# Sample attention: key pages waited for by halves, value pages released and loaded in two parts

## The chip, the cores and the metric

The kernel runs on one core of a Trainium2 chip. Its time is the device time of one execution in microseconds (us); the time before is 2310.9 us, the median of three runs (2310.64 to 2313.34). The engines are TensorE (PE in the profile, its weight loads PEld), VectorE (DVE), ScalarE (ACT), GpSimd (POOL) and SyncE (SP). An "SPq" row is SP issuing a transfer; POOL issues transfers too.

## The reference, cut to what matters

One decoder layer over a prompt of 1024 tokens and a sample group of 8 sequences with 8 new tokens each. The change concerns the attention of the sample group: each sequence attends to 1024 cached rows (8 pages of 128 rows, found through a page table) and its 8 new ones, over 8 heads of 64.

```python
k_past = cache_k[l][page_table].reshape(Bs, -1, ATT_HEADS, HEAD_DIM)
v_past = cache_v[l][page_table].reshape(Bs, -1, ATT_HEADS, HEAD_DIM)
...
s = jnp.einsum('bqhd,bkhd->bhqk', q, k).astype(jnp.float32) * (HEAD_DIM ** -0.5)
s = s + jnp.transpose(dq, (0, 2, 1))[..., None] - jnp.transpose(dk, (0, 2, 1))[:, :, None, :]
s = jnp.where(mask, s, -jnp.inf)
p = jax.nn.softmax(s, axis=-1)
return jnp.einsum('bhqk,bkhd->bqhd', p.astype(v.dtype), v)
```

dq and dk are running sums of a forget gate. Everything else in the layer (a combined input projection, a gated convolution, causal pooling, the gates, the output projection, two layer norms and a SwiGLU) is large matrix products and element work, and it is the same in both kernels.

## The kernel before, in words

The program is written engine by engine; each engine's list of instructions is fixed, and semaphores tie the lists together. Phases in order of time: set-up and modulation (to about 80 us), the prompt's attention with its projections (to about 472 us), the sample attention (472 to 665 us), and from there on matrix products of split float32 numbers, which keep TensorE busy to the end.

The sample attention goes sequence by sequence, b = 0 to 7; turns 0 to 6 are a hardware loop, turn 7 is written out. For each sequence there are four things in memory: `kpage` (8 key pages of 128x512), `kt_s` (the keys transposed), `decs` (the decay terms, then scores, then probabilities, 128 x 520) and `vpage` (8 value pages and the 8 new rows). All of them have one buffer. In turn b, TensorE does in this order:

1. the scores of b from `kt_s` (L1788);
2. groups 0 to 4 of the transposes of the keys of b + 1 (L1777; a group is four 128x128 transposes into one of two PSUM banks, even groups are copied out by ScalarE, odd ones by VectorE, L889 and L1233). Groups 0 to 3 read pages 0 to 3 (the first half), groups 4 to 7 pages 4 to 7;
3. the transposes of the probabilities of b (L1796, L1798), which wait for the softmax;
4. group 5;
5. the values of b: 8 matrix products over pages (L1809) and one over the new rows (L1810);
6. groups 6 and 7, then the fold of the heads (L1815).

The softmax of b is on VectorE: add and maximum (L1240), three small ones (L1243 to L1245), then `queries` of b + 1 (L1227, L1229) and the copies of groups 1 and 3, then the sum of the rows and the scaling (L1253 to L1257). ScalarE copies group 0, does the exponential (L895) and copies groups 2 and 4.

SP loads, per turn of its own loop: the first half of the key pages of a sequence after groups 0 to 3 of the one before, four decay transfers (L476) after the probabilities were transposed, and the second half of the key pages after group 7 of the one before. Both halves count on one semaphore, `kpg_in`, and TensorE waits before group 0 and again before group 4, both times for all eight pages. POOL loads all eight value pages (L366) and the new rows (L656) of b + 1 once the values of b are done (`ov_done`); TensorE waits for all of them before L1809. Before its loop POOL also splits the prompt's attended values (L631, L632).

Of the kernel before, what the change touches and what calls it, by code (L numbers as in the profile page):

```python
# [33 lines left out]
DB, DS = 8, 8  # L34
NS = DB * DS
T = 1092
TU = NP + NS
# [3 lines left out]
HP = H // 2  # L41
PAST, PAGE = 1024, 128
NPG = PAST // PAGE
# [4 lines left out]
NT = HALF // P  # L48
# [50 lines left out]
def build(nc, a, out):  # L99
    with ExitStack() as ctx:  # L100
# [167 lines left out]
        def scratch(name, shape):  # L268
# [14 lines left out]
            z_done e_done lf_done lf_tr lf_copied lfs_out lfnew_in scan_done ndp_out nds_out early_out  # L283
            q_done k_done v_done qhi_done ql_done kv_done kl_done tok_tr tok_copied kst vst vl_done decay0_in decay1_in
            s_done mx_done p_done pn_done tr_done pth_done ptl_done o_done o_copied ol_done
            kpg_in vpg_in dec_in vnew_in kt_tr kt_act kt_dve qbd_zero qbd_done ss_done sm_done se_done sp_done
            pt_tr pt_act pt_dve ov_done om_done fold_done sah_done sal_done pad_done
            cb_done cc_done ch_done cc_copied u_done y_done chi_done clo_done ul_done ul_tr ul_copied ul_out
            pcopied pf_done phi_done plo_done pt2_tr pt2_copied pt2_out mhi_done mlo_done
            wo_ev xr0_in xr1_in ysum_done mean_done d_done sq_done var_done sd_done xn_done xa_done  # L290
# [67 lines left out]
        def apart(eng):  # L358

            eng.sem_inc(s["idle"], 1)  # L360
# [18 lines left out]
        def _(sp):  # L379
# [73 lines left out]
            wunit(U_BRA + 2, (U_BRA + 2) % RING, tiles(a["w_br_attn"][0], 0, 2 * P), 4)  # L453

            sp.wait_ge(s["s_done"], NTILE * (HP - 1))
            for half in range(2):
                page_loads(sp, 0, kpage, "cache_k", s["kpg_in"], range(4 * half, 4 * half + 4))
            sp.wait_ge(s["o_copied"], NTILE * HP)
            sp.wait_ge(s["vl_done"], HP)
            sp.wait_ge(s["vst"], 32 * HP)  # L460
# [4 lines left out]
            def key_loads(b, half):  # L465
                sp.wait_ge(s["kt_tr"], b * 2 * HP - HP * (1 - half))
                apart(sp)
                page_loads(sp, b, kpage, "cache_k", s["kpg_in"], range(4 * half, 4 * half + 4))

            def decay_loads(b):  # L470
                if not isinstance(b, int) or b:
# [82 lines left out]
        def _(pool):  # L554
# [96 lines left out]
            nc.gpsimd.memset(qbd[:, :], 0.0).then_inc(s["qbd_zero"], 1)  # L651

            pool.wait_ge(s["pt_in"], 16)
            def sample_values(b):
                page_loads(pool, b, vpage, "cache_v", s["vpg_in"])
                pool.dma_start(vpage[0:DS, NPG, :],  # L656
                               out["v_sample"][0, bass.ds(b, 1)].rearrange("o t h d -> t (o h d)")).then_inc(s["vnew_in"], 16)

            sample_values(0)
            for p in range(HP):  # L660
                attended(p)
            with pool.Fori(1, DB) as b:
                pool.wait_ge(s["ov_done"], b)
                apart(pool)
                sample_values(b)
            one(U_BRA + 2)
            three(U_BRA + 3, (U_POOL - U_BRA - 3) // 3)
            for u_ in range(U_POOL, U_POOL + 4):
# [36 lines left out]
        def _(act):  # L705
# [176 lines left out]
            act.wait_ge(s["o_done"], HP * QT)  # L882
            act.wait_ge(s["kst"], 32 * HP)
            act.wait_ge(s["vst"], 32 * HP)
            nc.scalar.copy(ahi[:, :, TU:T], zeros[:, :].rearrange("p (a b) -> p a b", a=NT)).then_inc(s["pad_done"], 1)

            def keys_t(b, g):
                act.wait_ge(s["kt_tr"], b * 2 * HP + (g + 1))
# [153 lines left out]
        def _(dve):  # L1042
# [172 lines left out]


            dve.wait_ge(s["o_copied"], NTILE * HP)
            V.tensor_copy(alo[:, :, TU:T], zeros[:, :].rearrange("p (a b) -> p a b", a=NT)).then_inc(s["pad_done"], 1)
            dve.wait_ge(s["qbd_zero"], 1)
            dve.wait_ge(s["kst"], 32 * HP)  # L1220
            dve.wait_ge(s["vst"], 32 * HP)
# [13 lines left out]
            def sample(b, more):  # L1235
                dve.wait_ge(s["dec_in"], b * 64 + 64)
                link(V.tensor_tensor(decs[:, KH:LR], decs[:, KH:LR], maskn[:, :], ALU.add))
                dve.wait_ge(s["ss_done"], b + 1)
                apart(dve)
                link(V.tensor_tensor_reduce(decs[:, :], flat(psA)[:, 0:LR], decs[:, :], 1.0, NEG, ALU.add, ALU.max,  # L1240
                                            rowmax[:, 0:1]))

                link(V.tensor_scalar(other[0:NS, :], rowmax[NS:2 * NS, 0:1], -1.0, None, ALU.mult))  # L1243
                link(V.tensor_scalar(other[NS:2 * NS, :], rowmax[0:NS, 0:1], -1.0, None, ALU.mult))
                V.scalar_tensor_tensor(out=negmax[:, 0:1], in0=rowmax[:, 0:1], scalar=-1.0, in1=other[:, :], op0=ALU.mult,  # L1245
                                       op1=ALU.min).then_inc(s["sm_done"], 1)
# [12 lines left out]
                V.tensor_copy(ptrs[0:DS, NPG // 2, :], psB[0:DS, 1, 0:P]).then_inc(s["pt_dve"], 1)  # L1259
                if more:  # L1260
                    keys_t(b + 1, 5)

                dve.wait_ge(s["ov_done"], b + 1)
# [258 lines left out]
        def _(pe):  # L1522
# [247 lines left out]
            def keys_t(b, groups):  # L1770
                for g in groups:
                    if g % HP == 0:
                        pe.wait_ge(s["kpg_in"], b * (16 * NPG) + 16 * NPG)
                    if g >= 2:
                        pe.wait_ge(s["kt_dve" if g % 2 else "kt_act"], b * HP + g // 2)
                    for j in range(4):
                        m = tr(mi[g % 2][:, j * P:(j + 1) * P], kpage[:, 4 * (g // HP) + j, (g % HP) * P:(g % HP + 1) * P], ident[:, :])  # L1777
                    m.then_inc(s["kt_tr"], 1)

            def sample(b, more):  # L1780
# [17 lines left out]
                tr(psB[0:DS, 1, 0:P], decs[:, KH:LR], ident[:, :]).then_inc(s["pt_tr"], 1)  # L1798
                if more:
                    keys_t(b + 1, [5])  # L1800
                pe.wait_ge(s["vpg_in"], b * (16 * NPG) + 16 * NPG)
                pe.wait_ge(s["vnew_in"], b * 16 + 16)
                pe.wait_ge(s["pt_act"], b + 1)
                pe.wait_ge(s["pt_dve"], b + 1)
                hpg = NPG // 2
                for g in range(hpg):
                    for half in range(2):
                        rows = slice(half * NS, (half + 1) * NS)
                        mm(psB[rows, 2, :], ptrs[:, g, rows], vpage[:, half * hpg + g, :], start=g == 0, stop=half == 0 and g == hpg - 1)  # L1809
# [31 lines left out]
            branch(0, U_BRA, (s["ss_done"], DB), (s["sal_done"], DB), ((s["sal_done"], DB), (s["ol_done"], HP), (s["pad_done"], 2)))  # L1841

            pe.wait_ge(s["mA"], 4)
            pe.wait_ge(s["mB"], 4)
# [168 lines left out]
```

## Time and profile before

| what | value |
|---|---|
| median of 3 runs | 2310.9 us |
| the profiled execution's own time | 2310.69 us |
| its span, first to last instruction | 2309.0 us |
| TensorE busy | 2106.8 us, 91% |
| VectorE, GpSimd, ScalarE busy | 35%, 27%, 16% |
| mean granted TensorE clock | 0.953 |

The page cuts the span in 40 slices of 57.7 us. TensorE's busy tenths are 9 nearly everywhere; the slices of the sample attention read 6, 7, 6, 8, and the granted clock is 8 in each of them, against 9 behind it. Busy shares are means over phases; what counts in the sample attention is who waits for whom inside a turn, and that is read from its own stretch of the trace.

### The profile page before, as it was taken

What the parts mean: (1) busy time and instruction counts of PE and PEld (TensorE: products, weight loads), DVE (VectorE), ACT (ScalarE), POOL (GpSimd) and SP (SyncE); (2) the same over time, 40 slices, a digit from 0 to 9 for tenths busy, and PEclk for the clock granted to TensorE, in tenths of its full rate; (3) what the DMA queues carried; (4) which work ended last, traced back from release to release, by engine and by line L of the source; (5) the groups of instructions that cost most, each with busy time, mean ns of one, the idle gap of its engine ahead of it and who ended that gap; (6) DMA issues with size and microseconds to landing.
All of it is one profiled execution on the core that took longest, in us unless ns stands there. A gap on an engine that the chain in (4) does not pass through costs nothing.

```text
span 2309.0 us, 32811 instructions
## 1 busy us (share of the span) xinstructions
PE 2106.8 (91%) x13074; PEld 1986.3 (86%) x13074; DVE 798.3 (35%) x1328; ACT 367.6 (16%) x645; POOL 627.3 (27%) x474
## 2 busy tenths in 40 slices
PE   3899999867689999999979999699999999999996
PEld 3788888644469999999979999499999999999996
DVE  1525445533210023212532154714342243422426
ACT  1424344321110000000110100500000000000003
POOL 4220210041222222222222234042222222222233
PEclk8899999688889999999989999799999999999998
DMA  7861112045621111111111122011111111111112
GB/s 246 298 197 47 38 47 75 1 156 180 208 78 46 46 37 46 37 46 45 34 38 46 39 92 66 10 46 46 45 39 43 45 45 45 45 37 45 46 37 78
DMA packets 172992, 164.06 MB, mean 71 GB/s; under 512 B 13438, under 2 KB 136786, under 8 KB 172779
## 3 DMA queue, kind: packets, MB, share of 16 engines
q1 hardware_dynamic: 152155, 132.47, 18.6%
q0 software_dynamic: 6656, 17.08, 2.3%
q10 hardware_dynamic: 14104, 13.43, 1.8%
q8 instruction: 56, 0.92, 0.2%
q14 instruction: 21, 0.17, 0.0%
HBM read 149.03 MB, written 14.03 MB: 71 GB/s over the span
## 4 chain that ended last, share of the span: by engine, by line
PE 83%; DVE 7%; SPq 3%; issue 2%; DMA 2%; ACT 2%; POOLq 0%; POOL 0%; ACTq 0%; DVEq 0%
PE psA L1537 11%; PE psA L1543 11%; PE psA L1541 11%; PE psB L1543 10%; PE psB L1541 10%; PE psB L1537 10%; PE psB L1635 2%; PE psB L1638 2%; PE psB L1639 2%; DMA kpage<-in_cache_k 2%; PE ps L1777 1%; PE psB L1809 1%; PE ps L1702 1%; PE psA L1719 1%; PE psA L1720 1%
## 5 line engine op out<-in xcount | busy, mean ns | idle before, releaser
L597 POOL CAST whi<-raw 128x1024 fp32r<-128x1024 f32 x139 | 147.4, 1060 | 1289.2 <-PE psA L1537 607.0
L598 POOL TENSOR_TENSOR wlo<-raw,whi 128x1024 fp32r<-128x1024 f32 x139 | 336.8, 2423 | 11.2
L1537 PE MATMUL psA<-hhi,whi 128*128 128x364 f32 x1176 | 267.4, 337 | 47.1 <-DVE hlo L1403 20.2
L1541 PE MATMUL psA<-hlo,whi 128*128 128x364 f32 x1176 | 264.7, 334 | 0.0
L1543 PE MATMUL psA<-hhi,wlo 128*128 128x364 f32 x1176 | 264.2, 334 | 0.0
L1537 PEld LDWEIGHTS psA<-hhi,whi 128*128 128x128 f32 x1176 | 208.5, 193 | 53.6 <-issue 39.8
L1543 PE MATMUL psB<-hhi,wlo 128*128 128x364 f32 x1056 | 233.3, 329 | 0.0
L1541 PE MATMUL psB<-hlo,whi 128*128 128x364 f32 x1056 | 233.2, 329 | 0.0
L1537 PE MATMUL psB<-hhi,whi 128*128 128x364 f32 x1056 | 232.2, 328 | 0.0
L1543 PEld LDWEIGHTS psA<-hhi,wlo 128*128 128x128 f32 x1176 | 208.8, 192 | 0.0
L1541 PEld LDWEIGHTS psA<-hlo,whi 128*128 128x128 f32 x1176 | 208.7, 192 | 0.0
L1543 PEld LDWEIGHTS psB<-hhi,wlo 128*128 128x128 f32 x1056 | 183.7, 188 | 0.0
L1537 PEld LDWEIGHTS psB<-hhi,whi 128*128 128x128 f32 x1056 | 183.1, 188 | 0.0
L1541 PEld LDWEIGHTS psB<-hlo,whi 128*128 128x128 f32 x1056 | 183.1, 188 | 0.0
L1423 DVE TENSOR_TENSOR ft<-psB,sil 128x1092 f32<-128x1092 f32 x22 | 28.5, 1296 | 412.6 <-PE psB L1543 397.0
L1009 ACT CAST ahi<-ft 128x1092 fp32r<-128x1092 f32 x22 | 24.3, 1107 | 473.2 <-PE psB L1543 312.5
L1537 PE MATMUL psA<-ahi,whi 128*128 128x364 f32 x366 | 81.8, 332 | 8.5 <-DVE alo L1373 8.5
L1635 PE MATMUL psB<-hhi,whi 128*128 128x364 f32 x240 | 84.7, 353 | 2.0 <-DVE qlo L1121 2.0
L1777 PE MATMUL ps<-ident,kpage 128*128 128x128 f32 x256 | 49.4, 357 | 36.7 <-DMA kpage<-in_cache_k 35.4
L1296 DVE TENSOR_TENSOR part<-psA,sg 128x1092 f32<-128x1092 f32 x8 | 10.4, 1296 | 209.4 <-PE psA L1543 209.4
L1541 PE MATMUL psA<-alo,whi 128*128 128x364 f32 x366 | 81.1, 330 | 0.0
L1543 PE MATMUL psA<-ahi,wlo 128*128 128x364 f32 x366 | 81.1, 330 | 0.0
(328 smaller groups left out, 3312.2 us busy)
## 6 DMA issues: line engine op xcount, KB each, us to landing
raw<-in_w_in SPq DMA_DIRECT2D x53, 512.0 KB, 3.9
ada<-in_ada_w SPq DMA_DIRECT2D x12, 2048.0 KB, 13.8
raw<-in_w_gate_up SPq DMA_DIRECT2D x44, 512.0 KB, 3.8
kpage<-in_cache_k SPq DMA_DIRECT2D x64, 256.0 KB, 3.6
vpage<-in_cache_v POOLq DMA_DIRECT2D x64, 256.0 KB, 4.0
raw<-in_w_down SPq DMA_DIRECT2D x22, 512.0 KB, 3.7
x_keep<-xt SPq DMA_DIRECT2D x1, 4368.0 KB, 18.0
xr<-x_keep ACTq DMA_DIRECT2D x8, 546.0 KB, 4.9
```

The lines of the kernel that those rows point to most:

```text
L597: link(nc.gpsimd.tensor_copy(whi[slot][:, 0:n, :], raw[slot][:, 0:n, :]))
L598: nc.gpsimd.tensor_tensor(wlo[slot][:, 0:n, :], raw[slot][:, 0:n, :], whi[slot][:, 0:n, :].bitcast(F32), ALU.subtract).then_inc(s["w_split ...
L1009: nc.scalar.copy(to, ft[k][:, :]).then_inc(s["fhi_done"], 1)
L1423: V.tensor_tensor(c3(ft[k][:, :]), cols(psB), c3(sil[k][:, :]), ALU.mult).then_inc(s["ft_done"], 1)
L1537: m = mm(ps[:, c, 0:CH], whi[slot][:, b, :], hi[:, k, c * CH:(c + 1) * CH], start=first, stop=False)
L1541: mm(ps[:, c, 0:CH], whi[slot][:, b, :], lo[:, k, c * CH:(c + 1) * CH], start=False, stop=False)
L1543: m = mm(ps[:, c, 0:CH], wlo[slot][:, b, :], hi[:, k, c * CH:(c + 1) * CH], start=False, stop=last)
L1635: m = mm(bank[:, 0:CH], whi[slot][:, k, :], hhi[:, k, at], start=k == 0, stop=False)
L1638: mm(bank[:, 0:CH], whi[slot][:, k, :], hlo[:, k, at], start=False, stop=False)
L1639: m = mm(bank[:, 0:CH], wlo[slot][:, k, :], hhi[:, k, at], start=False, stop=k == KD - 1)
L1702: m = tr(mi[g % 2][:, j * P:(j + 1) * P], prob[n % 2][:, kb * P:(kb + 1) * P], ident[:, :])
L1777: m = tr(mi[g % 2][:, j * P:(j + 1) * P], kpage[:, 4 * (g // HP) + j, (g % HP) * P:(g % HP + 1) * P], ident[:, :])
```

## The change

The key pages get two semaphores, one for each half. TensorE waits for the first before group 0 and for the second before group 4. SP's order of transfers stays as it is.

The value pages get two parts. The products over pages 0, 4, 1, 5 come first (as before), and after them TensorE increments `ov_done` once, waits for `vnew_in`, does those over pages 2, 6, 3, 7 and the new rows, and increments `ov_done` again. POOL loads the first part of the next sequence after the first increment and the second part, with the new rows, after the second. The first part counts on `vpg_in`, the rest on `vnew_in`. Waits on `ov_done` elsewhere count twice. A semaphore for two writes of zeros is merged into another one.

```diff
-                page_loads(sp, b, kpage, "cache_k", s["kpg_in"], range(4 * half, 4 * half + 4))
+                page_loads(sp, b, kpage, "cache_k", s["kpg1_in" if half else "kpg_in"], range(4 * half, 4 * half + 4))
...
-            def sample_values(b):
-                page_loads(pool, b, vpage, "cache_v", s["vpg_in"])
+            V_FIRST, V_SECOND = (0, 1, 4, 5), (2, 3, 6, 7)
+
+            def values_first(b):
+                page_loads(pool, b, vpage, "cache_v", s["vpg_in"], V_FIRST)
+
+            def values_second(b):
+                page_loads(pool, b, vpage, "cache_v", s["vnew_in"], V_SECOND)
                 pool.dma_start(vpage[0:DS, NPG, :],
                                out["v_sample"][0, bass.ds(b, 1)].rearrange("o t h d -> t (o h d)")).then_inc(s["vnew_in"], 16)
...
             with pool.Fori(1, DB) as b:
-                pool.wait_ge(s["ov_done"], b)
+                pool.wait_ge(s["ov_done"], b * 2 - 1)
                 apart(pool)
-                sample_values(b)
+                values_first(b)
+                pool.wait_ge(s["ov_done"], b * 2)
+                apart(pool)
+                values_second(b)
...
                     if g % HP == 0:
-                        pe.wait_ge(s["kpg_in"], b * (16 * NPG) + 16 * NPG)
+                        pe.wait_ge(s["kpg1_in" if g else "kpg_in"], b * (8 * NPG) + 8 * NPG)
...
-                pe.wait_ge(s["vpg_in"], b * (16 * NPG) + 16 * NPG)
-                pe.wait_ge(s["vnew_in"], b * 16 + 16)
+                pe.wait_ge(s["vpg_in"], b * (8 * NPG) + 8 * NPG)
                 pe.wait_ge(s["pt_act"], b + 1)
                 pe.wait_ge(s["pt_dve"], b + 1)
                 hpg = NPG // 2
                 for g in range(hpg):
+                    if g == 2:
+                        m.then_inc(s["ov_done"], 1)
+                        pe.wait_ge(s["vnew_in"], b * (8 * NPG + 16) + 8 * NPG + 16)
```

No instruction changes its place on TensorE. In the loop's turn, from group 4 of the keys to the last value product, TensorE's list before is:

```order
L1775 REGISTER_ALU [waits kpg_in]
L1777 MATMUL ps<-ident,kpage 128x128 [waits kt_act]
L1796 MATMUL psB<-ident,decs 128x128 [waits sp_done]
L1798 MATMUL psB<-ident,decs 8x128
L1777 MATMUL ps<-ident,kpage 128x128 [waits kt_dve]
L1802 ISA [waits vpg_in]
L1809 MATMUL psB<-vpage,ptrs 64x512 [waits pt_dve,pt_act,vnew_in]
L1809 MATMUL psB<-vpage,ptrs 64x512 x7
L1810 MATMUL psB<-vpage,ptrs 64x512
```

and in the changed kernel (kpg1_in is the second half of the key pages, sp_done the finished probabilities):

```order
L1784 REGISTER_ALU [waits kpg1_in]
L1786 MATMUL ps<-ident,kpage 128x128 [waits kt_act]
L1805 MATMUL psB<-ident,decs 128x128 [waits sp_done]
L1807 MATMUL psB<-ident,decs 8x128
L1786 MATMUL ps<-ident,kpage 128x128 [waits kt_dve]
L1820 MATMUL psB<-vpage,ptrs 64x512 [waits pt_dve,pt_act,vpg_in]
L1820 MATMUL psB<-vpage,ptrs 64x512 x3
L1820 MATMUL psB<-vpage,ptrs 64x512 [waits vnew_in]
L1820 MATMUL psB<-vpage,ptrs 64x512 x3
L1821 MATMUL psB<-vpage,ptrs 64x512
```

The wait for the new rows moved from before the first value product to before the fifth, and the wait ahead of group 4 is on the second half alone. On POOL, the loop's turn before begins with its only wait (the eight transfers differ in nothing but the page, two are shown):

```order
L365 ISA [waits ov_done]
L365 TENSOR_LOAD ptab
L366 ISA
L366 DMA vpage<-in_cache_v 128x512
L366 DMA vpage<-in_cache_v 128x512
L656 DMA vpage<-out_v_sample 8x512
```

and now the same wait stands a second time, ahead of the fifth transfer:

```order
L365 ISA [waits ov_done]
L365 TENSOR_LOAD ptab
L366 DMA vpage<-in_cache_v 128x512
L365 ISA [waits ov_done]
L365 TENSOR_LOAD ptab
L366 DMA vpage<-in_cache_v 128x512
L661 DMA vpage<-out_v_sample 8x512
```

## Rows read from the trace of the kernel before

**Rows 1.** The page: busy us, share of the span, instructions.
```profile
PE 2106.8 (91%) x13074; PEld 1986.3 (86%) x13074; DVE 798.3 (35%) x1328; ACT 367.6 (16%) x645; POOL 627.3 (27%) x474
```

**Rows 2.** Waits, 465 to 665 us: engine line <- releaser: us, times, longest.
```profile
PE ps L1777 <- DMA kpage<-in_cache_k: 35.4, 7, 6.5
```

**Rows 3.** The chain that ended last: start us, us, what.
```profile
489.21 3.88 PE ps L1777 x16
...
515.50 3.65 PE ps L1777 x16
...
532.91 4.92 DMA kpage<-in_cache_k
537.88 3.88 PE ps L1777 x16
...
560.57 3.88 PE ps L1777 x16
...
579.59 5.80 DMA kpage<-in_cache_k
585.44 3.88 PE ps L1777 x16
...
630.61 3.88 PE ps L1777 x16
```

**Rows 4.** Timeline of the second turn: start, us, engine, instruction, count, [idle <- releaser].
```profile
506.96 4.07 PE L1788 MATMUL psA<-kt_s,qbd 128*64 128x512 f32 x32
...
511.23 0.70 DVE L1240 CUSTOM_DVE_ANT_0 decs<-psA,decs 128x520 f32<-128x520 f32 x1 [3.25 <-PE psA L1788]
...
512.87 0.18 DVE L1229 COPY kt_s<-k_s 128x32 f32 x1
...
515.50 4.24 PE L1777 MATMUL ps<-ident,kpage 128*128 128x128 f32 x20 [4.47 <-DMA kpage<-in_cache_k]
...
519.17 0.69 DVE L1233 COPY kt_s<-ps 128x512 f32<-128x512 f32 x1 [0.97 <-PE ps L1777]
...
520.66 0.49 DVE L1257 TENSOR_SCALAR decs<-decs,stat 128x520 f32<-128x520 f32 x1
...
521.29 0.63 PE L1796 MATMUL psB<-ident,decs 128*128 128x128 f32 x4 [1.55 <-DVE decs L1257]
...
522.64 3.65 PE L1809 MATMUL psB<-vpage,ptrs 128*64 128x512 f32 x16 [0.17 <-ACT ptrs L901]
...
526.23 1.07 PE L1810 MATMUL psB<-vpage,ptrs 8*64 8x512 f32 x2
```

**Rows 5.** Timeline ahead of the loop: two copies of key groups without another wait.
```profile
473.46 0.69 DVE L1233 COPY kt_s<-ps 128x512 f32<-128x512 f32 x1
...
474.89 0.69 DVE L1233 COPY kt_s<-ps 128x512 f32<-128x512 f32 x1 [0.75 <-PE ps L1777]
```

**Rows 6.** Timeline of SP's queue in the second turn.
```profile
520.04 3.84 SPq L366 DMA_DIRECT2D kpage<-in_cache_k  x4
...
524.25 3.05 SPq L476 DMA_DIRECT2D decs<-nd_s  x4
```

**Rows 7.** Timeline: last value product of turn 6, and POOL's last issue for turn 7.
```profile
641.57 1.07 PE L1810 MATMUL psB<-vpage,ptrs 8*64 8x512 f32 x2
...
653.26 0.52 POOL L656 DMA_DIRECT2D vpage<-out_v_sample  x1
```

**Rows 8.** Timeline of the last sequence.
```profile
653.47 0.59 ACT L901 COPY ptrs<-psB 128x512 f32<-128x512 f32 x1 [2.56 <-PE psB L1796]
...
656.07 6.64 PE L1809 MATMUL psB<-vpage,ptrs 128*64 128x512 f32 x16 [2.42 <-DMA vpage<-out_v_sample]
```

**Rows 9.** Stretches: us, busy us of each engine, PEclk, DMA share, GB/s.
```profile
511.00:515.00 4.00, 0.03 (x1) 0.00 (x0) 1.66 (x8) 0.00 (x0) 1.61 (x3) 1.00 1.00 365
...
515.00:537.80 22.80, 15.98 (x95) 9.51 (x95) 6.86 (x21) 3.84 (x8) 4.83 (x9) 0.88 0.62 201
...
560.50:585.40 24.90, 17.99 (x95) 10.63 (x95) 6.97 (x21) 3.83 (x8) 5.36 (x10) 0.77 0.58 190
```

More of the change, by code:

```diff
@@ L285, in build @@
             s_done mx_done p_done pn_done tr_done pth_done ptl_done o_done o_copied ol_done
-            kpg_in vpg_in dec_in vnew_in kt_tr kt_act kt_dve qbd_zero qbd_done ss_done sm_done se_done sp_done
-            pt_tr pt_act pt_dve ov_done om_done fold_done sah_done sal_done pad_done
+            kpg_in kpg1_in vpg_in dec_in vnew_in kt_tr kt_act kt_dve qbd_zero qbd_done ss_done sm_done se_done sp_done
+            pt_tr pt_act pt_dve ov_done om_done fold_done sah_done sal_done
             cb_done cc_done ch_done cc_copied u_done y_done chi_done clo_done ul_done ul_tr ul_copied ul_out
@@ L455, in _ @@
             sp.wait_ge(s["s_done"], NTILE * (HP - 1))
-            for half in range(2):
-                page_loads(sp, 0, kpage, "cache_k", s["kpg_in"], range(4 * half, 4 * half + 4))
+            for half, loaded in enumerate((s["kpg_in"], s["kpg1_in"])):
+                page_loads(sp, 0, kpage, "cache_k", loaded, range(4 * half, 4 * half + 4))
             sp.wait_ge(s["o_copied"], NTILE * HP)
@@ L653, in _ @@
             pool.wait_ge(s["pt_in"], 16)
-            def sample_values(b):
-                page_loads(pool, b, vpage, "cache_v", s["vpg_in"])
+            V_FIRST, V_SECOND = (0, 1, 4, 5), (2, 3, 6, 7)
[3 more added lines that the diff above has]
+                page_loads(pool, b, vpage, "cache_v", s["vnew_in"], V_SECOND)
                 pool.dma_start(vpage[0:DS, NPG, :],
                                out["v_sample"][0, bass.ds(b, 1)].rearrange("o t h d -> t (o h d)")).then_inc(s["vnew_in"], 16)
-            sample_values(0)
+            values_first(0)
+            values_second(0)
             for p in range(HP):
@@ L884, in _ @@
             act.wait_ge(s["vst"], 32 * HP)
-            nc.scalar.copy(ahi[:, :, TU:T], zeros[:, :].rearrange("p (a b) -> p a b", a=NT)).then_inc(s["pad_done"], 1)
+            nc.scalar.copy(ahi[:, :, TU:T], zeros[:, :].rearrange("p (a b) -> p a b", a=NT)).then_inc(s["ol_done"], 1)
             def keys_t(b, g):
@@ L1217, in _ @@
             dve.wait_ge(s["o_copied"], NTILE * HP)
-            V.tensor_copy(alo[:, :, TU:T], zeros[:, :].rearrange("p (a b) -> p a b", a=NT)).then_inc(s["pad_done"], 1)
+            V.tensor_copy(alo[:, :, TU:T], zeros[:, :].rearrange("p (a b) -> p a b", a=NT)).then_inc(s["ol_done"], 1)
             dve.wait_ge(s["qbd_zero"], 1)
@@ L1261, in sample @@
                     keys_t(b + 1, 5)
-                dve.wait_ge(s["ov_done"], b + 1)
+                dve.wait_ge(s["ov_done"], b * 2 + 2)
                 V.tensor_tensor(om[:, :].rearrange("p (h d) -> p h d", h=H), psB[:, 2, :].rearrange("p (h d) -> p h d", h=H),
@@ L1806, in sample @@
                 for g in range(hpg):
+                    if g == 2:
+                        m.then_inc(s["ov_done"], 1)
+                        pe.wait_ge(s["vnew_in"], b * (8 * NPG + 16) + 8 * NPG + 16)
                     for half in range(2):
                         rows = slice(half * NS, (half + 1) * NS)
-                        mm(psB[rows, 2, :], ptrs[:, g, rows], vpage[:, half * hpg + g, :], start=g == 0, stop=half == 0 and g == hpg - 1)
+                        m = mm(psB[rows, 2, :], ptrs[:, g, rows], vpage[:, half * hpg + g, :], start=g == 0, stop=half == 0 and g == hpg - 1)
                 mm(psB[rows, 2, :], ptrs[0:DS, hpg, rows], vpage[0:DS, NPG, :], start=False, stop=True).then_inc(s["ov_done"], 1)
@@ L1839, in branch @@
                                  begin=k == 0, free=((s[f"sg{x}"], i + (4 * j + 1)),))
-            branch(0, U_BRA, (s["ss_done"], DB), (s["sal_done"], DB), ((s["sal_done"], DB), (s["ol_done"], HP), (s["pad_done"], 2)))
+            branch(0, U_BRA, (s["ss_done"], DB), (s["sal_done"], DB), ((s["sal_done"], DB), (s["ol_done"], HP + 2)))
             pe.wait_ge(s["mA"], 4)
```

## The prediction

> **What bounds the kernel now.** The busy shares come first: TensorE works 91% of the span [rows 1], so a gain must come from its idle time, in the stretch that the change touches. That is the sample attention, where the view of waits names one releaser above all: the first key transposes of a turn wait for the key pages 7 times, 35.4 us together [rows 2]. Seven is the number of turns that have a next sequence. The chain that ended last shows that these waits are on the path and not beside it: each turn passes through the landing of the last key page, the fourth issue of the second half plus 4.92 us in one turn and 5.80 us in another, and goes on with L1777 [rows 3]. The starts of L1777 behind the landings give the turns: 26.29, 22.38, 22.69, 24.87 us, and the last two are 45.17 us together, 22.6 each [rows 3].
>
> The timeline of the second turn shows what the wait holds up [rows 4]. Scores end at 511.03 (506.96 + 4.07). TensorE then stands for 4.47 us until 515.50, though groups 0 to 3 need only pages 0 to 3. VectorE is through with the maximum and the queries at 513.05, and then waits too: its copies of groups 1 and 3 stand ahead of the normalising in its list. The copy of group 3 ends at 519.86, the scaling L1257 at 521.15, and the transposes of the probabilities start at 521.29, which is 10.26 us after the scores. From there to the end of the turn nothing waits long.
>
> **Key pages by halves, seven turns.** The second half's landing does not move against the scores: SP issues it after group 7 of the turn before, and TensorE's work from group 7 to the end of the scores is unchanged. It lands at 515.50 in the frame of this turn, and the wait ahead of group 4 stays there. What goes is that groups 0 to 3 wait for it.
>
> - Group 0 can start at 511.03. ScalarE copies it while VectorE is at the maximum.
> - The copy of group 1 can start when VectorE comes free, at 513.05. From the copy of group 1 to that of group 3 it takes 1.43 us when nothing else waits (473.46 to 474.89) [rows 5]. So group 3 is copied from 514.48 to 515.17.
> - From the end of that copy to the end of L1257 it took 1.29 us (519.86 to 521.15) [rows 4]: 516.46. The transposes start 0.14 us behind, at 516.60, instead of 521.29. That is 4.69 us earlier.
> - Group 4 wants the landing, 515.50, and about 0.5 us (16 transposes took 3.65 us with their waits, four take less than a quarter of that): done at 516.0, 0.6 us ahead of what it could hold up.
>
> So two chains end within 0.6 us of each other: VectorE's at 516.60 and the key pages' at 516.0. In four other turns the 16 transposes took 3.88 us instead of 3.65 [rows 3], so 0.2 us may go to slower copies: 4.5 us left. If the landing takes 5.80 us [rows 3] instead of this turn's 4.8, group 4 ends at 517.0 and 4.3 us are left. I take 4.5 us a turn, the middle of the bounds 4.3 and 4.7. Seven turns: 31.5 us. The turn becomes 22.4 - 4.5 = 17.9 us.
>
> Does SP keep up with that? Its issues of a first half take 3.84 us from 520.04 and the decay transfers 3.05 us from 524.25 [rows 6]. Group 3 comes 4.3 us earlier, so these run from 515.8 to 522.8; the second half is asked for at 532.91 - 3.50 - 4.6 = 524.8. SP is free 2 us before. The first half issued by 519.6 lands 5 us later, 4 us before the next turn's group 0 (511.03 + 17.9 = 528.9).
>
> **Value pages in two parts.** POOL's chain can be read at the last sequence: the products of turn 6 done at 642.64 (641.57 + 1.07), POOL's last issue at 653.26, start of the last turn's products at 656.07: 13.4 us in all [rows 7, 8]. With the release at the end of L1810 (4.66 us after the first product, 522.64 to 527.30 [rows 4]) the turn can't be shorter than 4.66 + 13.4 = 18.1 us, just above the 17.9. The first release now comes after half of the products, 2.7 us earlier (522.64 + 1.83, with about 0.15 for the last to drain, against 527.30), and the last part is wanted 1.8 us later. The bound falls to about 13.6 us and is gone. So this half of the change is worth 0.2 us a turn, already in the 17.9.
>
> It is worth more in the last sequence, which has no key wait. There the probabilities are copied by 654.06 and the products wait until 656.07 for the value pages [rows 8]. The first part has landed long before, the second lands 2.7 us earlier than 656.0. Start of the products at 654.15: 1.9 us gained.
>
> **What is added.** Eight waits of TensorE between the fourth and fifth product. Where the pages have landed such a wait costs next to nothing; no row shows it, and I bound it by 0 and by the 0.17 us that TensorE stood ahead of L1809 for ScalarE's copy [rows 4], 1.4 us for all eight; I take 0, since the first products are still draining. Behind it on TensorE are the other products, groups 6 and 7 and so the second half of the key pages; it would matter if the second part landed late. It lands 13.4 us after the release, 15.4 us after the first product, and is wanted 17.9 + 1.8 us after it: 4 us in hand. POOL's second wait has behind it five transfers. It is met 2.7 us after the first, before the fourth issue is out (nine issues took 10.6 us from the release, 1.2 us each), so it holds nothing. The merged semaphore costs nothing.
>
> **Sum.** 31.5 + 1.9 = 33.4 us off the profiled execution's own 2310.69 us: 2277.3 us. The median of the runs is 0.2 us above that execution: 2277.5, told as 2277 us.
>
> **The rivals.** (a) *The clock comes back as well.* In the fourth turn the granted clock was 0.77 where it was 0.88 in the second, and the turn took 24.87 instead of 22.6 us; the last sequence's products took 6.64 us where the second turn's took 3.65 [rows 3, 4, 8, 9]. Each time TensorE had stood idle before at full clock and went on at the low level. With the key wait gone the fall may not come: 2.3 + 3.0 us more, and some in the first turn, 2271 us. The Trainium skill says this in "TensorE: Matmul & The Clock Gate", section "HAM oscillation — how this bites in real kernels": a transfer waited for between short bursts throttles the array again each time. The rows agree for the waits that there are; against it, the rest of VectorE's chain still leaves TensorE idle some 3 us a turn (5.6 us less five groups of 0.5), and the last sequence, which has no groups, all 5.6 less its start.
>
> (b) *The clock stays low longer*, since short work between gaps replaces one gap: five more turns like the fourth, 5 x 2.3 = 11.5 us, 2289 us.
>
> (c) *The two streams get in each other's way.* While both run, the transfers are at their limit: DMA share 1.00 and 365 GB/s in the stretch where the second key half lands [rows 9]. The value pages now start 2.7 us earlier against the scores, so up to four of them (1 MB, 2.9 us at 365 GB/s) can be ahead of the key pages. If all that falls on the key landing, it comes at 518.4, the transposes at 518.9, and 2.4 us of the 4.7 are left: 17 + 1.9, 2292 us. Against it: value issues (a page of 128x512x4 bytes in 1.2 us, 218 GB/s) alone don't fill the engines, so there is no pile when the key issues begin; over a turn 16 pages and 0.26 MB of decay terms, 4.5 MB, take 12.3 us at 365 GB/s, of 17.9. I expect landings of 4.7 to 5.8 us still. The Trainium skill, "DMA: Bandwidth & Descriptors", section "Issuing engines are not separate DMA queues", speaks for (c): transfers from all engines run on the same 16 and interleave. The full share in the rows agrees.
>
> (d) *Slower.* The same mechanism grown: group 4 holds the probabilities' transposes beyond 521.29 once the second key half lands after 520.8, which is 10.1 us behind its last issue (4.8 us before 515.50) instead of 4.8. If it took 11.6 us, each turn would be 1.5 us longer than before, 10.5 us less 1.9: 2319 us. It would take more than twice the landing time that the same two streams show now.
>
> (e) *It doesn't do what it says*: group 0 waits as long as before, because its first half, issued behind other transfers on SP's queue, lands no earlier than the second. Then the last sequence's 1.9 us are all: 2309 us. Against it: the first half is issued from 520.04 on [rows 6], more than 10 us before the second and ahead of the decay transfers, and wanted only after the next scores.
>
> **Chances.** Forecast 0.60 (own range 2273 to 2282); (a) 0.15; (b) 0.09; (c) 0.11; (d) 0.02; (e) 0.03. The range that holds 8 in 10 reaches over (a) and most of (b): 2269 to 2290 us. 0.2% of the time is 4.6 us, about what a measurement can tell from no change: faster by more 0.95, within 0.03, slower by more 0.02.
>
> **What would show it.** Turns of 17.5 to 18.2 us between the probabilities' transposes; the key transposes waiting for pages ahead of group 4 for under 1.5 us a turn and not ahead of group 0; 5.6 us from the end of the scores to the transposes; the largest idle time of TensorE ahead of the transposes, for VectorE's scaling; the value products waiting for no page, in the last sequence either. I am wrong if the key landing is above 6.5 us behind its last issue, if the clock in these turns is below 0.8, or if the matrix products behind the loop change their time.

## The result and the profile after

The changed kernel takes 2269.4 us (median of four runs, 2267.9 to 2274.8) beside 2310.8 us before; the ratio is 0.9823, 95% interval 0.9805 to 0.9840. Run again later it took 2274.3 us beside 2309.7 us, ratio 0.9843 (0.9822 to 0.9864). So it is faster by 35 to 41 us. The forecast was 2277 us, 33 us faster.

The profiled execution took 2274.75 us of its own with a span of 2273.1 us. To see where the time went, the span is cut at two marks: POOL's clearing of `qbd`, with which the sample attention begins, and the first matrix product of the gates behind it. I did the same for every kernel below (us, one profile each):

| kernel | up to the stage | sample attention | rest | span | median of runs |
|---|---|---|---|---|---|
| before | 472.3 | 193.1 | 1643.6 | 2309.0 | 2310.8 |
| changed | 471.0 | 160.3 | 1641.8 | 2273.1 | 2269.4 |
| changed, again | 470.4 | 156.4 | 1642.1 | 2269.0 | 2274.3 |
| value half only | 468.9 | 190.4 | 1645.8 | 2305.0 | 2307.0 |
| key half only | 472.1 | 180.3 | 1639.2 | 2291.6 | 2293.3 |
| key half only, with filler | 472.6 | 177.2 | 1642.4 | 2292.2 | 2296.0 |
| both, early release only | 469.2 | 156.6 | 1641.8 | 2267.7 | 2270.4 |
| both, split wait only | 473.6 | 160.8 | 1641.5 | 2275.9 | 2277.3 |
| before, with filler | 468.6 | 184.1 | 1642.2 | 2294.8 | 2298.5 |
| changed, queries late | 473.3 | 153.2 | 1642.2 | 2268.7 | 2268.5 |
| changed, pages read ahead | 472.4 | 156.6 | 1645.6 | 2274.5 | 2276.2 |
| changed, with filler | 470.3 | 151.6 | 1643.7 | 2265.6 | 2265.2 |
| queries late and filler | 467.7 | 149.8 | 1642.2 | 2259.7 | 2263.7 |

The columns beside the stage differ by 6 to 7 us between executions whose work there is the same. That is this kernel's noise. I read the stage wherever a few us matter, but it has a spread of its own: the one kernel that was profiled twice took 160.3 and 156.4 us there. A difference of up to 4 us between the stages of two single profiles shows nothing by itself. The changed kernel ran in the first set and beside the two halves and the filler in the kernel before; the other experiments ran on another chip, where it was not run again, and with them whole times are compared by their ratios to the kernel before.

The waits of the changed kernel, 460 to 640 us (the last of the rows is idle time before the probabilities' transposes; it answers to [rows 2]):

```profile
PE ps L1786 <- DMA kpage<-in_cache_k: 11.4, 8, 3.0
...
PE psB L1805 <- DVE decs L1266: 8.7, 5, 3.7
```

35.4 us of waiting for key pages have become 11.4. Of these, 8.4 us are ahead of group 4, 0.5 to 2.0 us a turn, and 3.0 us are ahead of group 0 in the first turn, which still waits there for its first half:

```profile
484.36 1.09 PE L1786 MATMUL ps<-ident,kpage 128*128 128x128 f32 x8 [2.98 <-DMA kpage<-in_cache_k]
```

The chain that ended last no longer goes through a landing in each turn. (A landing is the end of a transfer.) Two turns of it, one that does and one that does not:

```profile
505.86 5.50 DMA kpage<-in_cache_k
511.49 1.11 PE ps L1786 x4
512.60 0.85 PE psB L1805 x4
...
514.52 4.93 PE psB L1820 x16
...
558.12 4.08 PE psA L1797 x30
...
564.20 0.61 DVE kt_s L1242
564.85 0.67 PE ps L1786 x4
...
567.03 0.50 DVE decs L1266
567.66 0.64 PE psB L1805 x4
...
569.01 3.65 PE psB L1820 x16
```

In the first the landing is the last thing, 5.50 us behind its issue, and TensorE goes on at the lower of its two clock levels: group 4 takes 1.11 us and the products 4.93, where the second turn has 0.65 and 3.65. In the second the chain is VectorE's, as forecast: its copy of group 1 waits for the queries, group 3 for that copy, and the scaling for the copy of group 3. The timeline of that turn answers to [rows 4]:

```profile
558.12 4.07 PE L1797 MATMUL psA<-kt_s,qbd 128*64 128x512 f32 x32
...
562.38 0.70 DVE L1249 CUSTOM_DVE_ANT_0 decs<-psA,decs 128x520 f32<-128x520 f32 x1 [3.06 <-PE psA L1797]
...
564.11 0.68 DVE L1242 COPY kt_s<-ps 128x512 f32<-128x512 f32 x1
...
565.54 0.69 DVE L1242 COPY kt_s<-ps 128x512 f32<-128x512 f32 x1 [0.75 <-PE ps L1786]
...
566.31 0.65 PE L1786 MATMUL ps<-ident,kpage 128*128 128x128 f32 x4 [0.80 <-DMA kpage<-in_cache_k]
...
567.66 0.63 PE L1805 MATMUL psB<-ident,decs 128*128 128x128 f32 x4 [0.70 <-DVE decs L1266]
```

From the end of the scores (562.19) to the probabilities' transposes it takes 5.47 us, where it took 10.26; the copies of groups 1 and 3 start 1.43 us apart; group 4 gets its page at 566.31, 1.35 us ahead of the transposes. The turn's length, from these transposes to the same of the turn before (550.22), is 17.44 us.

The stretches show the clock that goes with each kind of turn (columns as in [rows 9]):

```profile
512.60:531.90 19.30, 17.12 (x95) 9.12 (x94) 6.79 (x21) 3.95 (x9) 4.84 (x9) 0.85 0.68 218
...
550.20:567.70 17.50, 14.76 (x96) 8.34 (x97) 6.77 (x21) 3.94 (x9) 4.83 (x9) 1.00 0.77 256
...
471.02:631.20 160.18, 129.56 (x760) 71.25 (x760) 60.00 (x168) 30.66 (x64) 52.68 (x81) 0.90 0.69 217
```

The whole stage had a granted clock of 0.83 before:

```profile
472.33:665.40 193.07, 136.38 (x760) 79.14 (x761) 60.27 (x168) 30.78 (x64) 52.45 (x81) 0.83 0.56 180
```

### The profile page after: what moved, and what is told of

It reads as the page before. It is cut to its first block, busy times and chain, and to the rows that moved or that the text cites. A ratio compares the mean times of both kernels' runs of the same rounds, so it can differ in the third digit from the quotient of the medians.

```text
span 2273.1 us, 32817 instructions
## 1 busy us (share of the span) xinstructions
PE 2095.0 (92%) x13074; PEld 1973.3 (87%) x13074; DVE 796.7 (35%) x1328; ACT 367.1 (16%) x645; POOL 628.0 (28%) x474
## 4 chain that ended last, share of the span: by engine, by line
PE 84%; DVE 7%; issue 2%; ACT 2%; SPq 2%; DMA 2%; ACTq 0%; POOLq 0%; POOL 0%; DVEq 0%
PE psA L1546 11%; PE psA L1552 11%; PE psA L1550 11%; PE psB L1552 10%; PE psB L1550 10%; PE psB L1546 10%; PE psB L1644 2%; PE psB L1647 2%; PE psB L1648 2%; PE psB L1820 2%; DMA ada<-in_ada_w 1%; PE ps L1711 1%; PE psA L1797 1%; PE ps L1786 1%; PE psA L1728 1%
## 5 line engine op out<-in xcount | busy, mean ns | idle before, releaser
L1546 PE MATMUL psB<-ahi,whi 128*128 128x364 f32 x366 | 81.0, 330 | 0.0
```

The source lines that it names most:

```text
L1546: m = mm(ps[:, c, 0:CH], whi[slot][:, b, :], hi[:, k, c * CH:(c + 1) * CH], start=first, stop=False)
```

## The experiments

**The same kernel again.** No edit.

> The changed kernel once more, unchanged, for its median beside the others and for a second profile. In the first profile the seven turns took 17.4 to 20.2 us, and the slow ones are those at a low granted clock (0.85 and 0.86 against 1.00). Theory A (the 5 to 7 us by which the other three runs were faster than the profiled one are turns at full clock): 2266 to 2270 us in the runs, and in the new profile the turns near 17.5 us have a clock of 1.00, the longer ones one below 0.93. Theory B (the difference lies outside the sample attention): the turns add up to the same 130 us while the whole is 5 us shorter.

Measured: 2274.3 us (2268.9 to 2277.6), stage 156.4 us. The turns from value product to value product were 19.3, 17.4, 17.5, 18.1, 19.0, 17.4 and 16.2 us. Between the probabilities' transposes the granted clock was 1.00 in the two turns of 17.4 us and 0.85 and 0.87 in the two longest (19.3 and 18.8 us), and the stage is 3.9 us shorter than in the first profile while the rest is the same. So theory A holds for the profile; its 2266 to 2270 us for the runs did not come (2274.3). B is not wrong either: the runs still spread over 9 us, and the table shows such a spread outside the stage. A run's few us above or below another are not explained by the turns alone.

**The two halves apart.** Value half only:

```diff
-                        pe.wait_ge(s["kpg1_in" if g else "kpg_in"], b * (8 * NPG) + 8 * NPG)
+                        pe.wait_ge(s["kpg_in"], b * (16 * NPG) + 16 * NPG)
```

(and both halves' loads count on `kpg_in`).

> Only the value pages' half: TensorE waits for all eight key pages before group 0 as before. Theory of the prediction: the key landing sets every turn as before, 22.4 to 22.7 us; only the last sequence starts its value products 1.9 us earlier: 2307 to 2310 us. Rival (value loads ahead of the key loads pile up before them): the second key half lands later than 4.9 us after its last issue, each us of it makes seven turns longer, 2315 us and more.

Measured: 2307.0 us, ratio 0.9987 (0.9972 to 1.0001), stage 190.4 us. The last landings and the last sequence in its chain of waits:

```profile
597.54 4.80 DMA kpage<-in_cache_k
602.39 3.88 PE ps L1786 x16
...
620.02 5.14 DMA kpage<-in_cache_k
625.21 3.88 PE ps L1786 x16
...
650.02 6.08 PE psB L1820 x16
```

The key landing sets the turns as before (22.8 us between these two) and comes no later: 3.7 to 5.9 us behind its last issue in all seven. In the last sequence the products begin 5.36 us after the maximum began (644.66), where it was 7.29 us before (648.78 to 656.07): 1.93 us, and no row waits for a value page. The stage's 2.7 us less agree; the interval of the whole time still holds 1. The rival of a pile-up is out.

Key half only:

```diff
-                pool.wait_ge(s["ov_done"], b * 2 - 1)
+                pool.wait_ge(s["ov_done"], b)
                 apart(pool)
                 values_first(b)
-                pool.wait_ge(s["ov_done"], b * 2)
-                apart(pool)
                 values_second(b)
...
                 pe.wait_ge(s["vpg_in"], b * (8 * NPG) + 8 * NPG)
+                pe.wait_ge(s["vnew_in"], b * (8 * NPG + 16) + 8 * NPG + 16)
...
-                    if g == 2:
-                        m.then_inc(s["ov_done"], 1)
-                        pe.wait_ge(s["vnew_in"], b * (8 * NPG + 16) + 8 * NPG + 16)
```

> Only the key pages' half: the value pages are released and waited for together as before. Theory of the prediction (POOL's chain of 13.4 us starts after the last value product, so a turn can't be shorter than 18.1 us; the last sequence waits for its value pages again): against the changed kernel's 17.45 us a full-clock turn 0.6 us more in up to seven turns and 1.9 us in the last sequence, 3 to 7 us slower than the changed kernel, 2272 to 2275 us; the value products wait for pages in every full-clock turn. Rival (the value part does nothing but in the last sequence): 2 us slower than the changed kernel. Rival (the early value loads take bandwidth from the key pages): faster than the changed kernel, with key landings below 5.2 us.

Measured: 2293.3 us, ratio 0.9925 (0.9906 to 0.9944): 19 us slower than the changed kernel on the same chip, stage 180.3 us. None of the expectations reaches that. Its chain:

```profile
532.37 4.62 DMA vpage<-out_v_sample
537.04 6.31 PE psB L1816 x16
...
554.98 3.99 DMA vpage<-out_v_sample
559.01 5.57 PE psB L1816 x16
...
641.07 2.77 DMA vpage<-out_v_sample
643.93 5.78 PE psB L1816 x16
```

The stretch of that turn:

```profile
537.04:559.01 21.97, 17.99 (x95) 9.23 (x95) 6.77 (x21) 3.82 (x8) 5.09 (x9) 0.81 0.56 190
```

Every turn is now POOL's: from the last product (543.28 + 1.07 = 544.35) to the next first one (559.01) it takes 14.66 us; the first six of the seven stretches of this kind are 14.6 to 16.4 us long, the one ahead of the last sequence 13.5. In five of them the new rows land 3.9 to 4.6 us behind their issue, while key pages come in, and 2.8 us in the last sequence, where none do. And the products behind that wait take 5.1 to 6.4 us at a low clock in six turns (3.65 in one).

Cut at the end of the products, the seven turns are 44.4 us of products and 104.0 us from their end to the next ones; in the first profile of the changed kernel they are 37.6 and 91.5 us. So of 19.4 us between the two, 12.5 lie in the stretch that POOL's chain now sets and 6.9 are products at a low clock.

**Is it the clock?** The key half with TensorE kept busy ahead of the wait, by transposes that nobody reads (filler, below); the diff is against the key half:

```diff
+                for _ in range(24):
+                    tr(psB[:, 2, 0:P], ident[:, :], ident[:, :])
                 pe.wait_ge(s["vpg_in"], b * (8 * NPG) + 8 * NPG)
```

> The kernel with the key pages' half only, and 24 transposes of the identity (nobody reads them, 2.7 us at full clock) on TensorE ahead of its wait for the value pages. That kernel was 19 us slower than the changed one where 3 to 7 were expected; its value products wait up to 3.2 us for the new rows and then take 5.1 to 6.4 us instead of 3.65. Clock theory: 1.5 to 2.5 us of each turn are the products at the low clock, behind that wait; with TensorE kept busy the products take 3.65 us, the turns 19.5 to 20 us instead of 21 to 22: 10 to 14 us faster than the key half alone, 2280 to 2284 us. Rival (POOL's chain of 14.7 us from the last product to the next first one and the products' own length set the turn, the clock follows from something else): no faster than 2291 us.

Measured: 2296.0 us, ratio 0.9953 (0.9938 to 0.9968), stage 177.2 us. The theory falls as stated: the products are at full clock in every turn but the kernel is no faster (0.9925 without the filler).

```profile
559.66 2.62 PE psB L1809 x24
562.28 3.58 PE psB L1818 x16
...
580.45 2.71 PE psB L1809 x24
583.16 3.58 PE psB L1818 x16
```

It is not a clean test either: in six turns the products start right behind the filler, with no wait for a page (0.5 us in all), so the filler took up what the clock gave. Its turns were 19.3 to 21.3 us; POOL's chain wants 4.65 + 14.7 = 19.3 us at full clock. The stage is 3 us shorter than without the filler, no more than two profiles of one kernel differ by. What the key half alone would take at full clock and without filler stays open.

**Early release or split wait?** Two kernels with both halves of the change, each without one piece of the value half. Release early, wait for all value pages ahead of the first product:

```diff
                         m.then_inc(s["ov_done"], 1)
-                        pe.wait_ge(s["vnew_in"], b * (8 * NPG + 16) + 8 * NPG + 16)
```

(the removed wait stands ahead of the first product).

> Both halves of the change, but TensorE waits for the second value part and the new rows ahead of the first value product again; the early release of the first part stays. The sample attention took 160 and 156 us in the two profiles of the changed kernel and 180 us with the key half alone. Threshold theory (POOL's chain from release to product is 14.7 us beside the key loads; a full-clock turn must be longer than the time from the first product to the release plus this chain, 2.0 + 14.7 = 16.7 us, and is 17.5): the early release alone gives nearly all of the value half, stage 157 to 162 us, 2270 to 2277 us. Rival (each of the two earns its own 2.7 and 1.8 us a turn): stage 168 to 172 us, 2282 to 2286 us.

Measured: 2270.4 us, ratio 0.9833 (0.9817 to 0.9850), stage 156.6 us, no wait for a value page. And the wait split, both parts loaded after the last product:

```diff
-                pool.wait_ge(s["ov_done"], b * 2 - 1)
+                pool.wait_ge(s["ov_done"], b * 2)
```

> Both halves of the change, but POOL loads both value parts only after the last value product, as before; TensorE's wait stays split. Threshold theory: the turn must be longer than 4.65 + 14.7 - 1.8 = 17.5 us, just what the full-clock turn is: stage 158 to 165 us, 2272 to 2280 us, waits of up to 1 us ahead of the fifth product in some turns. Rival (each earns its own): stage 171 to 175 us, 2285 to 2289 us.

Measured: 2277.3 us, ratio 0.9860 (0.9842 to 0.9877), stage 160.8 us, with TensorE's weight loads waiting for the new rows 3.0 us in four turns, 1.6 us in one of them where up to 1 was expected:

```profile
PEld psB L1820 <- DMA vpage<-out_v_sample: 3.0, 4, 1.6
```

The threshold theory holds on both, the additive rival on neither. Without both pieces the stage is 180 us, with the early release 157, with the split wait 161, with both 156 or 160. What counts is whether POOL's chain fits into the turn: 19.3 us does not fit into 17.4, 17.5 just does, 16.7 does easily. The early release alone does as much as both; the split wait alone is 7 us slower in the runs (2268.6 to 2274.3 us against 2276.9 to 2279.0, on one chip), though its stage is within the spread.

**What the key wait cost beyond its own length.** The kernel before, kept busy while it waits:

```diff
                 m.then_inc(s["ss_done"], 1)
+                for _ in range(32):
+                    tr(psB[:, 0, 0:P], ident[:, :], ident[:, :])
                 if more:
```

> The kernel before with 32 transposes of the identity (nobody reads them) on TensorE between the scores and the first key group of each sequence, about 3.5 of the 4.5 us that it waits there for key pages. Clock theory: part of the key wait's cost is that TensorE goes on at the low clock behind it. Kept busy it goes on at full clock: 0.5 to 0.8 us a turn, 2.3 us in the fourth, about 2 in the first and 3.0 in the last sequence, 8 to 12 us in all: 2299 to 2303 us, granted clock above 0.95 in the turns. Rival (the landing alone sets the turn, the clock is beside it): 2309 to 2312 us.

Measured: 2298.5 us, ratio 0.9947 (0.9927 to 0.9967), 11 us faster than before, 0.5 us beyond the range that was expected; stage 184.1 us, 9 us less. The clock theory holds. The second turn:

```profile
507.16 3.71 PE L1792 MATMUL psB<-ident 128*128 128x128 f32 x32
...
512.31 1.09 PE L1777 MATMUL ps<-ident,kpage 128*128 128x128 f32 x8 [1.44 <-DMA kpage<-in_cache_k]
...
517.00 0.63 PE L1798 MATMUL psB<-ident,decs 128*128 128x128 f32 x4 [1.37 <-DVE decs L1257]
```

TensorE still waits for the landing, but from there to the transposes it takes 4.69 us instead of 5.79 [rows 4]. So of the changed kernel's 33 to 37 us in the stage some 9 could have been had without moving a wait. The changed kernel takes only part of them: its granted clock in the stage is 0.90, this one's 0.96.

**What bounds the changed kernel.** VectorE's queries moved behind the copy of group 5:

```diff
                 if more:
-                    queries(b + 1)
                     keys_t(b + 1, 1)
                     keys_t(b + 1, 3)
...
                     keys_t(b + 1, 5)
+                    queries(b + 1)
```

> The changed kernel with VectorE's queries of the next sequence (L1236, L1238, about 0.6 us) moved from ahead of the copies of groups 1 and 3 to behind the copy of group 5. Theory (in full-clock turns VectorE's chain ends last, the copy of group 1 waits for the queries): the transposes of the probabilities come 0.3 to 0.6 us earlier in such turns, since the key landing (group 4 at 566.31 of a turn whose transposes start at 567.66) leaves 0.7 us: 2 to 3 us faster than the changed kernel, 2270 to 2273 us beside its 2274. Rival (the key landing ends last in most turns): no difference, and the wait for key pages ahead of group 4 grows.

Measured: 2268.5 us, ratio 0.9830 (0.9810 to 0.9850), stage 153.2 us, 3 to 7 us less than the changed kernel's; by the ratios (0.9823 and 0.9843 for the changed kernel) the whole time is not told apart from it. Four turns are 16.9 to 17.2 us and one 17.6, and in the chain each goes through the key landing:

```profile
526.52 4.59 DMA kpage<-in_cache_k
...
533.21 3.65 PE psB L1820 x16
...
543.47 4.91 DMA kpage<-in_cache_k
...
550.36 3.65 PE psB L1820 x16
```

The step to the landing's chain is 0.4 us a turn, inside the 0.3 to 0.6 that were expected. This kernel also waits longer ahead of group 4, 1.5 to 2.3 us in these five turns, and goes on at full clock:

```profile
548.50 0.65 PE L1786 MATMUL ps<-ident,kpage 128*128 128x128 f32 x4 [1.86 <-DMA kpage<-in_cache_k]
```

So the 1.6 to 2.0 us of wait ahead of group 4 in the changed kernel's slow turns are not by themselves what takes the clock down. In its second profile group 4 is at the low clock behind waits of 1.06 us. Why some turns fall and others do not stays open.

Then the landing itself, with SP's page numbers read ahead of the wait:

```diff
+                if half:
+                    pages = [sp.value_load(...) for g in range(4, 8)]
+                    sp.wait_ge(s["kt_tr"], b * 2 * HP)
+                    ...
```

> The changed kernel with SP's four page numbers of the second key half read ahead of its wait, so that the four issues follow each other by about 0.4 us instead of 1.17. Theory (the slow turns of the changed kernel are those in which the second key half lands over 5 us after its last issue, TensorE stands 1.9 us ahead of group 4 and goes on at the low clock): the landing comes 1 to 2 us earlier, the wait ahead of group 4 is under 0.5 us, no turn but the first is above 18 us: 3 to 6 us faster, 2268 to 2271 us. Rival (the transfers' rate is the limit, 1 MB beside the value pages): the landing behind the last issue grows by what the issues gain, and nothing is won.

Measured: 2276.2 us, ratio 0.9858 (0.9834 to 0.9882), stage 156.6 us, no gain. SP's queue and two landings in the chain:

```profile
533.51 3.05 SPq L484 DMA_DIRECT2D decs<-nd_s  x4
539.85 1.89 SPq L472 DMA_DIRECT2D kpage<-in_cache_k  x4
```

```profile
541.41 6.48 DMA kpage<-in_cache_k
...
576.83 5.82 DMA kpage<-in_cache_k
```

The four issues take 1.9 us instead of 3.8, and the landing behind the last grows to 5.8 and 6.5 us, as the rival said. But the edit did less than it was meant to. SP is busy with the decay transfers until 536.56 and reads the four page numbers only then, while group 7 ends at 537.58:

```profile
536.49 1.09 PE L1794 MATMUL ps<-ident,kpage 128*128 128x128 f32 x8
```

So it issues from 539.85 on, and the last issue comes 3.8 us behind group 7 where it came 4.6 us behind it in the changed kernel: 0.8 us were gained, not 1.9. The landing is 10.3 us behind group 7 here, 9.0 to 10.1 us there. That it does not move is shown; that the transfers' own rate is the limit is not, for the DMA share was 0.81 to 0.84 from 540 to 546 us and full only in the last 1.9 us.

**The rest of the clock, and the two together.** Filler in the changed kernel:

```diff
                 if more:
-                    keys_t(b + 1, range(5))
+                    keys_t(b + 1, range(4))
+                for _ in range(8 if more else 32):
+                    tr(psB[:, 0, 0:P], ident[:, :], ident[:, :])
+                if more:
+                    keys_t(b + 1, [4])
```

> The changed kernel with 8 transposes of the identity on TensorE ahead of group 4 of each turn (0.9 us at full clock, where it waits 0.8 to 2 us) and 32 of them (3.5 us) behind the scores of the last sequence. Clock theory: the last sequence's value products take 3.65 us instead of 5.1 to 5.5 and the transposes ahead of them 0.4 less (2 us), and the turns that fell to the low clock stay near 17.5 us (up to 2 us each in two or three of them): 3 to 7 us faster than the changed kernel, 2267 to 2271 us. Rival (the clock falls for gaps spread over the turn, not for the one ahead of group 4): 2 us, from the last sequence alone.

Measured: 2265.2 us, ratio 0.9818 (0.9796 to 0.9839), stage 151.6 us, 5 to 9 us less, at a granted clock of 0.97 there instead of 0.90. By the ratios (0.9823 and 0.9843) the whole time is again not told apart from the changed kernel's. The last sequence:

```profile
610.40 3.71 PE L1803 MATMUL psB<-ident 128*128 128x128 f32 x32
...
614.20 0.63 PE L1809 MATMUL psB<-ident,decs 128*128 128x128 f32 x4
...
615.55 3.65 PE L1824 MATMUL psB<-vpage,ptrs 128*64 128x512 f32 x16 [0.61 <-ACT ptrs L910]
```

Its products take 3.65 us, 5.08 in the first profile of the changed kernel. With the queries late as well:

> The changed kernel with both of the edits that made it faster: the queries behind the copy of group 5 and the transposes of the identity (8 ahead of group 4, 32 in the last sequence). With the queries moved the turns were 16.9 to 17.6 us and the key landing ended last in seven; with the filler the stage lost the low clock but kept turns of 17.5. If the two add: turns of 17.0 us at clock 1.00, last sequence at full clock, stage 147 to 149 us against 153.2 and 151.6 with one each, 2261 to 2264 us. If the key landing holds both back (its last issue is tied to group 7 of the turn before): stage 150 to 152 us, no faster than the filler alone.

Measured: 2263.7 us (2257.5 to 2270.1), ratio 0.9801 (0.9779 to 0.9823), stage 149.8 us: just above the 147 to 149 for adding up, and at the edge of the other. The intervals of this one and of the filler alone overlap, so that it is the fastest of all is not shown. In the stage both single profiles are 5 to 10 us below the two of the changed kernel.

## Why the prediction was right, and where it was not

- *The key landing is on the path, and what goes is that groups 0 to 3 wait for it.* Right. The stage is 32.8 us shorter in the profiled execution and 36.6 in the second profile; the forecast sum was 33.4. Cut at the probabilities' transposes of turn 6, the part with the seven key waits is 31.1 and 33.6 us shorter (forecast 31.5) and the rest 1.7 and 3.0 us (forecast 1.9).
- *5.6 us from the scores to the transposes, turns of 17.9 us, copies 1.43 us apart.* 5.47 us, 17.44 us and 1.43 us in a turn at full clock. The forecast of the turn started from 22.4, which held some low-clock time. Only two turns of the first profile are that short; the others took 17.9 to 20.0 us.
- *Two chains within 0.6 us.* Right in kind: VectorE's ends last in full-clock turns, by 0.7 us behind group 4, and once it was shortened the landing took over. What the sum did not price is that some turns fall to the low clock: three of 19.5 to 20 us in the first profile and two of some 19 in the second, 6.7 and 3.4 us more than the same turns at 17.4. The wait ahead of group 4 alone does not decide which.
- *The value half, 0.2 us a turn and 1.9 us in the last sequence.* The last sequence is right to the tenth (1.93 us). The term for the turns is the step that failed: beside the key half the value half is worth 20 to 24 us of the stage, not the 3.3 us that the prediction gave it (0.2 us a turn and 1.9). The 13.4 us of POOL's chain were read in the one sequence that has no key loads; beside them it is 14.6 to 16.4. Added to 4.66 it gives at least 19.3 us where turns of 17.4 were on offer, and behind that wait come products at a low clock, 6.9 us more of them in all. The total came out right because the sum priced the key half as if the values never held it, which is true only with the other half in: the share of each half was wrong, the two together were not.
- *SP and the added waits.* SP kept up, with 1.0 us in hand in a full-clock turn (free at 556.21, group 7 done at 557.24) where 2 were forecast. No turn of the changed kernel waits for a value page.
- *Two readings of the rows.* [rows 3] shows five turns at 3.88 us, not four, and in rival (e) the first half is issued 9.4 us before the second (520.04 and 532.91 - 3.50), not more than 10. Neither moves the sum.
- *The signs.* The products behind the loop kept their time and no value product waits. But the wait ahead of group 4 was above 1.5 us in three turns of the first profile, group 0 still waited 3.0 us in the first turn, and the largest idle time of TensorE is the one for key pages (11.4 us), not the one for the scaling (8.7).
- *Rival (a), the clock comes back.* In part: the granted clock is 0.90 in the stage after 0.83, with single turns at 1.00, and the last sequence's products take 5.1 and 5.5 us after 6.6. The median is nearer its 2271 than to 2277 in the first set, 2274 in the second lies between; how much of that is the clock is not shown. Of the 41 us of the first set the profiled execution has 36, and 33 of these lie in the stage; where the other runs gained the rest no profile shows.
- *Rivals (b) to (e).* None was seen. Where the key landing decided, it came 5.2 to 5.5 us behind its last issue (4.6 in the second profile). That is what was expected and far from the 7.7 us of (c); the 1 MB of value pages issued ahead did not fall on it.

## What to carry to other kernels

Two changes that each remove a wait from the same loop don't have prices of their own: find the length at which the loop would run without the wait, and ask of every other chain whether it fits into that. A chain's length is to be read where its neighbours run too, since the transfer that lands in 2.8 us in the last sequence takes 3.9 to 4.6 beside the key pages. And a wait of TensorE can cost more than its own length where the clock falls behind it. Filler in the wait shows how much, in one run, as long as it ends before the wait does: in the key half alone it outlasted the wait and showed nothing. One profile of each kernel was enough for differences of 9 us and more here, and not for 4.

## What the runs showed of the hardware

- Behind all seven key waits of the kernel before (4.5 to 6.5 us) TensorE's granted clock was 0.50, the lower of its two levels, for the next 2.4 us. In two of these turns the low clock reached the value products (4.9 and 4.3 us instead of 3.65), and behind the last sequence's wait for value pages they took 6.6 us. Behind shorter waits it fell in some turns only: behind 1.06 us in two turns of the changed kernel's second profile, and not behind 1.5 to 2.3 us in five turns of the kernel with the queries late.
- Transposes that nobody reads, put into the wait, kept the granted clock at 0.99 from the second turn of the kernel before on: the stage was 9 us shorter in the kernel before (11 us in its runs), and 5 to 9 us in the changed one, by one profile each.
- The 16 KB of new rows landed 2.8 us behind their issue in the last sequence and 3.9 to 4.6 us behind it in five turns in which key pages came in (the key half alone).
- Four page loads of 256 KB issued in 1.9 us instead of 3.8 landed no earlier while POOL's value pages were coming in: 5.8 and 6.5 us behind the last issue instead of 5.2 to 5.5. The last issue came only 0.8 us earlier.
